# Expert rounds of 32 tokens over four column groups of TensorE, weights in twelve 8 KB ring slots

## The chip, the core and the metric

The kernel runs on one core of one Trainium2 chip. A core has TensorE (PE, with its weight loads listed apart as PEld), VectorE (DVE), ScalarE (ACT), GpSimd (POOL) and SyncE (SP), which here does nothing but issue the transfers of the weights. Everything is float32. The metric is the device time of one execution in microseconds, lower is better.

## What is computed

The reference applies two blocks to 256 tokens of width 1024 (the first block also reads 256 context tokens). Each layer mixes tokens (three kinds of attention-like mixers) and then runs a mixture of experts. There are 32 experts in 4 groups of 8; every token goes to the two best experts of its best group. The first block has one layer, the second has two, so there are three expert phases. Cut to what matters here:

```python
# first block: EXPERT_HIDDEN = 512, two experts of 32 for each of 256 tokens
def expert_block(args):
    xb, e = args
    g, u = jnp.split(xb @ w_up[e], 2, axis=-1)      # 1024 x 1024 weights
    return (jax.nn.silu(g) * u) @ w_down[e]          # 512 x 1024 weights
y = y[dest] * gate ; segment_sum over the tokens
# second block, twice: D_EXPERT = 256, the same choice of two out of 32
hid = jax.nn.silu(t @ w_gate[g, e]) * (t @ w_up[g, e]) * combine   # 1024 x 256 each
y = y + hid @ w_down[g, e]                                         # 256 x 1024
```

All experts' weights are read once in each phase: 32 x 6.29 MB = 201.3 MB in the first block and 32 x 3.15 MB = 100.7 MB in each layer of the second. How many tokens an expert has follows from the inputs and decides how often an expert is run. Worked out from the reference with its own inputs (experts 0 to 31 in order):

| phase | tokens of each expert |
|---|---|
| first block | 2 0 4 1 3 2 7 7 8 6 12 3 0 6 6 7 **37** 20 12 13 7 4 1 0 **129** 14 **40** 2 **108** 29 13 9 |
| second block, layer 1 | 32 14 18 25 20 29 23 1 15 9 12 18 2 6 12 10 28 9 8 7 22 7 17 6 29 19 15 6 5 **36 38** 14 |
| second block, layer 2 | **43** 27 28 **57 54** 25 **33 33** 9 7 14 6 1 8 5 12 6 2 5 5 12 0 6 12 11 22 7 12 5 24 3 18 |

## The kernel before

The program of each engine is written out by hand with semaphores between them. SP streams all weights of the kernel, in the order of their use, through a ring of six slots of 16 KB per partition (2 MB each, 12.6 MB in all). It may refill a slot once PE has counted up `piece_used` for it (`expert_loads`, L452 to L467).

An expert phase (`experts_pe`, `experts_act`, `experts_dve`) is a loop. `batch_of` gives its shape: in the first block a turn takes 2 experts with 64 token places each (16 turns), in the second 4 experts with 32 places each (8 turns a layer). In a turn, DVE makes a 0/1 matrix that picks the tokens (L1090) and its product with the gates (L1096). PE gathers the tokens with four 512-column matmuls (L941), turns the result by eight transposes (L948, L957), and multiplies with up and gate weights (L979). There the tokens are stationary, 64 or 32 columns of the array for each expert, and the weights stream past in 512 columns, so two or four experts share the array side by side. ACT applies silu (L1045), DVE multiplies (L1115), PE transposes the hidden values (L990) and runs the down matmuls (L1006). The results go back to the tokens by four `combine` matmuls (L929), which add into four PSUM banks through the whole phase; they are one round late and sit between the other steps.

An expert with more tokens than places is run again before its main round with the same weights (`each_batch`; the number of extra rounds is loaded from SBUF into a register, L899, and a loop runs over them). In the first block an extra round is for one expert with 128 places; in the second it covers all 4 experts of the turn. By the table there are 2 extra rounds in the first block (experts 24 and 28), 1 in layer 1 and 2 in layer 2 of the second: 37 rounds with the 32 main ones.

A weight piece of a turn is one slot: 4 pieces of up (or gate and up), 2 of down. Each is released by the last matmul that reads it, in the main round.

Of the kernel before, what the change touches and what calls it, by code (L numbers as in the profile page):

```python
# [17 lines left out]
ALU = mybir.AluOpType  # L18
# [3 lines left out]
P = 128  # L22
D = 1024
# [3 lines left out]
SLOT = 4096  # L27
RING = 6
# [3 lines left out]
GRID = 64  # L32
BIG = 1e30
# [119 lines left out]
SEMS = """params loaded_x loaded_ctx loaded_bias bias_out piece0 piece1 piece2 piece3 piece4 piece5 piece_used  # L153
# [6 lines left out]
w_sel w_g0 w_g1 w_ct w_ct_sb w_comb_sb w_up w_silu w_hid w_ht0 w_ht1 w_y w_got_s w_got_v w_gt0 w_gt1 w_xg_v w_xg_s w_ysb_s w_ysb_v w_selg p2_mm p2_s p2_v st_mm pool_w head_s head_v final_gain moe_mm  # L160
fin_x
cq_sq cq_mean cq_sqrt cq_n cq_T cq_Ts q_mm q_sb kv_mm kv_sb head_T 
st_zb st_ln st_x st_a st_T st_Ts st_pv st_o pool_d pool_ds pool_y pool_o
w_hsb0 w_hsb1 const2 params2 written scale lam lam_sums lam_exp router_w zero_tile ranked w_cur c_used """.split()
# [33 lines left out]
class Ring:  # L198
# [5 lines left out]
    def place(self, dmas):  # L204

        slot = self.n % RING
        self.n += 1
        self.loads[slot] += 16 * dmas
        return slot, self.sems[f"piece{slot}"], self.loads[slot]

    def loop(self, turns, per_turn, dmas, dmas_down):

        assert per_turn == RING
        out = []
        for j in range(per_turn):
            slot, step = (self.n + j) % RING, 16 * (dmas if j < 4 else dmas_down)
            out.append((slot, self.sems[f"piece{slot}"], self.loads[slot], step))
            self.loads[slot] += step * turns
        self.n += turns * per_turn
        return out  # L220
# [20 lines left out]
def hybrid_kernel(nc, ins, out):  # L241
# [6 lines left out]
    with ExitStack() as ctx:  # L248
# [5 lines left out]

        ring = sb("ring", RING * SLOT).rearrange("p (r n) -> p r n", r=RING)
        X = sb("X", NT * D).rearrange("p (t d) -> p t d", t=NT)
# [79 lines left out]
        comb_next = arena[:, 13056:13312]  # L336
        cur = work[:, 768:784]
        silu_sb, hid = work[:, 784:1296], work[:, 1296:1808]
        hidT = work[:, 1808:2320].rearrange("p (c n) -> p c n", c=4)
        gotT = work[:, 2320:3344].rearrange("p (k n) -> p k n", k=KD)  # L340
        got = arena[:, 11008:12032]
        y_sb = arena[:, 12032:13056]
# [3 lines left out]
        ranks = rt[:, 0:128].rearrange("p (r e) -> p r e", e=NE)  # L346
# [70 lines left out]
        def w_cols(slot, width):  # L417

            return ring[:, slot, 0:KD * width].rearrange("p (k n) -> p k n", k=KD)

        def start_piece(sp, slot, sem, piece, layer):
# [13 lines left out]
            elif kind in ("wout", "wout2"):  # L435
                w = ins["w_out"][0] if kind == "wout" else ins["w_out_2"][layer]
                sp.dma_start(ring[:, slot, 0:4 * D].rearrange("p (k n) -> p k n", k=4),
                             w[512 * j:512 * j + 512, :].rearrange("(k p) n -> p k n", p=P)).then_inc(sem, 16)
            elif kind == "mla":
                sp.dma_start(ring[:, slot, 0:1536].rearrange("p (k n) -> p k n", k=2),  # L440
                             ins["w_uq_2"][layer].rearrange("(k p) n -> p k n", p=P)).then_inc(sem, 16)
                sp.dma_start(ring[:, slot, 1536:2560], ins["w_ukv_2"][layer]).then_inc(sem, 16)

        up1 = ins["w_expert_up"][0].rearrange("(b e) (k p) n -> b p e k n", e=2, p=P)
        down1 = ins["w_expert_down"][0].rearrange("(b e) (k p) n -> b p e k n", e=2, p=P)

        def expert_loads(sp, plan, which, ups, down):

            nb, _, hidden = batch_of(which)
            base, turns = plan.n, NE // nb  # L450
            slots = plan.loop(turns, RING, 2, hidden // P // 2)
            with sp.Fori(0, turns) as turn:  # L452
                for j, (slot, sem, _, _) in enumerate(slots):

                    sp.wait_ge(sems["piece_used"], turn * RING + (base + j - RING + 1))
                    if j < 4:
                        v = piece_view(slot, which, False)
                        for u, src in enumerate(ups):
                            if which == 2:
# [1675 lines left out]
```

## Time and profile before

| | |
|---|---|
| median of 3 runs | 1836.61 us (1832.91 to 1839.12) |
| profiled execution, its own time | 1836.74 us |
| span of its trace | 1835.0 us |
| PE busy | 1550.9 us (85%) |
| DVE, ACT busy | 453.4 us, 400.8 us |
| weights moved by SP's queue | 468.61 MB |
| first block's experts | from 391.96 us, last combine from 943.73 us |
| second block's experts, layer 1 | from 1118.05 us, last combine from 1377.61 us |
| second block's experts, layer 2 | from 1541.91 us, last combine from 1814.98 us |

The span runs from the first to the last instruction. A fp32 matmul shows as two records for PE (and two for PEld), a transpose as one. "x64" behind a row is the number of such records merged in it; a row's duration covers them all. The ends of matmuls are modelled, so distances between starts are the surer measure.

### The profile page before, as it was taken

How to read it: one execution, taken by the hardware profiler on the slowest of the kernel's cores; microseconds unless marked ns; L12 is line 12 of the kernel's file. 1: busy time of each engine (PE TensorE's matmuls, PEld its weight loads, DVE VectorE, ACT ScalarE, POOL GpSimd, SP SyncE). 2: the span in 40 equal slices, each digit the busy share in tenths (PEclk: the TensorE clock that was granted, in tenths of full speed). 3: DMA queues.
4: the chain of work that ended last, by engine and by line, in shares of the span. 5: the costliest groups of instructions: out<-in, count | busy, mean ns of one | idle time of the engine just before them, and what ended most of it. 6: DMA issues, size and time to landing. Idle time of an engine off the chain costs nothing.

```text
span 1835.0 us, 20256 instructions
## 1 busy us (share of the span) xinstructions
PE 1550.9 (85%) x7433; PEld 705.2 (38%) x7434; DVE 453.4 (25%) x1278; ACT 400.8 (22%) x778; POOL 41.7 (2%) x80
## 2 busy tenths in 40 slices
PE   3999987889999999999979788777788887888674
PEld 2555444343333333333327444222226544332221
DVE  0103356432121212121222513111112523121111
ACT  1101224122222222222222412121212412222111
POOL 2000201000000000000000000000000000000000
PEclk9899969979999999999989888897999997998888
DMA  9857300229999999858582224999975321779995
GB/s 319 308 200 276 114 2 1 105 87 405 410 410 410 410 410 410 344 220 329 220 331 92 92 97 163 397 392 396 393 263 212 138 63 45 275 283 392 395 393 205
DMA packets 174249, 477.30 MB, mean 260 GB/s; under 512 B 8465, under 2 KB 18958, under 8 KB 174014
## 3 DMA queue, kind: packets, MB, share of 16 engines
q1 hardware_dynamic: 171136, 468.61, 66.9%
q0 software_dynamic: 2160, 6.51, 1.3%
q10 hardware_dynamic: 910, 1.59, 0.3%
q8 instruction: 29, 0.48, 0.1%
q14 instruction: 14, 0.11, 0.0%
HBM read 474.71 MB, written 1.97 MB: 260 GB/s over the span
## 4 chain that ended last, share of the span: by engine, by line
PE 66%; DMA 14%; DVE 8%; SPq 7%; issue 2%; ACT 2%; ACTq 0%; DVEq 0%; POOL 0%
PE psum L979 16%; DMA ring<-in_w_down 10%; PE psum L1006 9%; PE psum L929 6%; PE psum L941 6%; SPq L460 6%; PE psum L1638 5%; PE psum L662 5%; PE psum L1634 3%; DMA ring<-in_w_up 2%; PE psum L1208 2%; PE psum L1196 2%; SPq L467 1%; PE psum L542 1%; PE psum L1242 1%
## 5 line engine op out<-in xcount | busy, mean ns | idle before, releaser
L979 PE MATMUL psum<-ring,arena 128*32 128x512 f32 (+2 forms) x2304 | 413.0, 635 | 64.0 <-DMA ring<-in_w_up 62.0
L979 PEld LDWEIGHTS psum<-ring,arena 128*32 128x32 f32 (+2 forms) x2304 | 124.4, 128 | 343.5 <-issue 290.6
L1006 PE MATMUL psum<-ring,arena 128*32 128x512 f32 (+2 forms) x1152 | 211.4, 640 | 52.0 <-DMA ring<-in_w_down 43.3
L929 PE MATMUL psum<-arena 128*128 128x512 f32 x320 | 169.4, 635 | 3.2 <-DVE arena L1069 3.2
L1115 DVE TENSOR_TENSOR arena<-arena,psum 128x256 f32<-128x256 f32 (+1 forms) x37 | 20.4, 551 | 502.5 <-ACT arena L1045 502.5
L941 PE MATMUL psum<-xn,arena 128*128 128x512 f32 x296 | 133.3, 593 | 1.5 <-DVE arena L1090 1.5
L1006 PEld LDWEIGHTS psum<-ring,arena 128*32 128x32 f32 (+2 forms) x1152 | 59.1, 127 | 173.3 <-issue 106.8
L1045 ACT ACTIVATE arena<-psum 128x256 f32<-128x256 f32 (+1 forms) x37 | 18.0, 487 | 411.3 <-PE psum L979 411.3
L1638 PE MATMUL psum<-ring,hT 128*128 128x512 f32 x224 | 97.7, 593 | 0.0
L929 PEld LDWEIGHTS psum<-arena 128*128 128x128 f32 x320 | 54.2, 197 | 100.8 <-issue 95.2
L1067 DVE COPY arena<-psum 128x512 f32<-128x512 f32 x40 | 27.6, 691 | 252.2 <-PE psum L929 252.2
L662 PE MATMUL psum<-ring,arena 128*128 128x512 f32 x192 | 86.0, 607 | 2.4 <-DVE arena L638 1.5
L941 PEld LDWEIGHTS psum<-xn,arena 128*128 128x128 f32 x296 | 56.7, 192 | 74.2 <-issue 71.1
L1031 ACT ACTIVATE arena<-psum 128x512 f32<-128x512 f32 x40 | 23.9, 597 | 214.7 <-PE psum L929 214.7
L1041 ACT ACTIVATE arena<-psum,small 128x128 f32<-128x128 f32 x148 | 48.7, 411 | 97.1 <-PE psum L957 97.1
L1638 PEld LDWEIGHTS psum<-ring,hT 128*128 128x128 f32 x224 | 41.9, 190 | 50.5 <-issue 50.5
L1031 ACT ACT_TABLE_LOAD x37 | 47.5, 1283 | 51.2 <-issue 45.4
L662 PEld LDWEIGHTS psum<-ring,arena 128*128 128x128 f32 x192 | 37.0, 195 | 50.3 <-issue 50.3
L1100 DVE COPY arena<-psum 128x512 f32<-128x512 f32 x37 | 25.6, 692 | 95.0 <-PE psum L941 95.0
L1634 PE MATMUL psum<-hT,ring 128*128 128x256 f32 (+2 forms) x144 | 47.4, 491 | 1.6 <-DVE hT L1913 1.3
L1045 ACT ACT_TABLE_LOAD x37 | 47.5, 1283 | 0.7
L753 PE MATMUL psum<-const_sb,xn 128*128 128x128 f32 x80 | 17.7, 413 | 34.3 <-DVE xn L724 34.3
(329 smaller groups left out, 1441.6 us busy)
## 6 DMA issues: line engine op xcount, KB each, us to landing
ring<-in_w_expert_up SPq DMA_DIRECT2D x128, 1024.0 KB, 9.8
ring<-in_w_expert_down SPq DMA_DIRECT2D x64, 1024.0 KB, 12.2
ring<-in_w_gate SPq DMA_DIRECT2D x64, 1024.0 KB, 14.2
ring<-in_w_up SPq DMA_DIRECT2D x64, 1024.0 KB, 14.3
ring<-in_w_down SPq DMA_DIRECT2D x32, 2048.0 KB, 16.8
ring<-in_w_mod SPq DMA_DIRECT2D x12, 2048.0 KB, 14.6
ring<-in_w_in SPq DMA_DIRECT2D x6, 2048.0 KB, 9.1
ring<-in_w_out SPq DMA_DIRECT2D x6, 2048.0 KB, 13.4
```

What stands on the lines that cost most here:

```text
L460: sp.dma_start(v[:, u], src[bass.ds(turn, 1)][0][:, :, 2 * j:2 * j + 2, :]).then_inc(sem, 16)
L662: mm = pe.matmul(ps[2 * t + n], mix[:, 4 * j + k, P * t:P * t + P], w[:, k, 512 * n:512 * n + 512], start=(j == 1 and k == 0), stop=(j == ...
L929: return pe.matmul(ps[4 + 2 * t + n], comb[:, P * t:P * t + P], y_sb[:, 512 * n:512 * n + 512], start=False, stop=True, skip_group_check=True)
L941: mm = pe.matmul(ps[2 + n], sel[:, t, :], xn[:, t, 512 * n:512 * n + 512], start=(t == 0), stop=(t == NT - 1))
L979: mm = pe.matmul(out_, gotT[:, k, its], rhs, start=(k == 0), stop=(k == KD - 1))
L1006: mm = pe.matmul(ps[n][its, :], hidT[:, k, its], view[:, e, kk, 512 * n:512 * n + 512], start=(k == 0), stop=(k == chunks - 1))
L1031: act.activation(y_sb[:, 0:512], ps[0], ACT.Copy).then_inc(sems["w_ysb_s"], 1)
L1041: ins_ = act.activation(gotT[:, k, :], ps[1][:, P * (k - 4):P * (k - 4) + P], ACT.Identity, scale=scale[:, k:k + 1], bias=0.0 if shift is ...
L1045: act.activation(silu_sb[:, 0:hidden], ps[2][:, 0:hidden], ACT.Silu).then_inc(sems["w_silu"], 1)
L1196: mm = pe.matmul(ps[4 + part][:, S * c:S * c + S], w[:, k, col:col + P], h2T[:, k, :], start=(k == 0), stop=(k == KD - 1))
L1634: mm = pe.matmul(bank[0:m, 0:tokens], w[:, k, col + P * i:col + P * i + m], hT[:, k, 0:tokens], start=(k == 0), stop=(k == KD - 1))
L1638: mm = pe.matmul(bank, hT[:, k, P * i:P * i + P], w[:, k, :], start=(k == 0), stop=(k == KD - 1))
```

## The change

The three expert phases get a new shape. A group is now 4 experts in every phase: one gather of 4 x 32 places for the group, whose 16 matmuls give the tokens' columns at once (no transposes). Within a group the first block runs 4 rounds of one expert, the second block 2 rounds of two. In a round the four 32-column groups of the array hold the same tokens (or two experts' tokens twice) and stream different quarters (halves) of the weights' columns: 32 up matmuls of 256 columns. The down matmuls are 16 of 256 columns, or 8 of 512. The four combine matmuls over all 128 rows become 8 over 32 rows each (first block) or 4 over 64 rows (second). A round has 32 places for each expert in all phases, and an extra round gathers anew for its own expert or pair.

The ring becomes twelve slots of 1 MB. A piece is one transfer: two weight rows of 4 KB per partition, or for gate and up of the second block 8 KB in one run per partition, where the old kernel's runs are 2 KB. In the first block a piece is released as before, by its last matmul; in the second, four at once after the up matmuls and combine, and two after the down matmuls.

```diff
-SLOT = 4096
-RING = 6
+SLOT = 2048
+RING = 12
+ROUND = 6
...
+        def each_round(eng, at, which, extra_round, main_round):
...
+            rounds = GROUP // experts_of(which)
             eng.wait_ge(*at("ranked"))
...
+            with eng.Fori(0, NE // GROUP) as turn:
+                for i in range(rounds):
+                    n = eng.value_load(extra[0:1, bass.ds(turn * rounds + i, 1)], min_val=0, max_val=7)
+                    begin = extra_round(turn, i, None)
                     with eng.If(n > 0):
...
                         with eng.Fori(0, n):
...
+                            extra_round(turn, i, True)
+                    main_round(turn, i)
...
+            def gather(select, width, out):
+
+                for k in range(KD):
+                    for t in range(NT):
+                        mm = pe.matmul(out(k)[:, 0:width], xn[:, t, P * k:P * k + P], select[:, t, 0:width],
+                                       start=(t == 0), stop=(t == NT - 1))
...
+            def combine():
+
+                w, wide = W * at_once, S * at_once
+                for t in range(NT):
+                    for n in range(P // w):
+                        r = slice(w * n, w * n + w)
+                        out_ = ps[4 + n][:, S * t:S * t + S] if which == 1 else ps[4 + 2 * t + n]
+                        mm = pe.matmul(out_, comb[r, P * t:P * t + P], y_sb[r, 0:wide], start=False, stop=True,
+                                       skip_group_check=True)
+                return mm
+
+            def up(turn, i, got, col, main):
...
+                            for j in range(4):
+                                mm = pe.matmul(out_(j), got[:, k, col:col + W], w[:, kk, :, j, :],
+                                               start=(k == 0), stop=(k == KD - 1))
+                        if main and piece < 3:
+                            mm.then_inc(sems["piece_used"], 1)
+                else:
+                    for piece in range(4):
+                        slot_ready(turn, ROUND * i + piece)
...
             def round_(turn, i, got, gates, col, main, ready):
...
                 pe.wait_ge(sems["w_comb_sb"], v + part)
...
+                combine_turn(gates, col)
+                if ready:
+                    pe.wait_ge(sems[ready[0]], ready[1])
+                up(turn, i, got, col, main)
+                pe.wait_ge(sems["w_ysb"], v + part)
+                combine()
+                if main and i == rounds - 1:
+                    gather_group()
                 pe.wait_ge(sems["w_hid"], v)
...
+                pe.transpose(U[:, 0:P], hid, ident).then_inc(sems["w_ht"], 1)
+                if main:
+
+                    pe.sem_inc(sems["piece_used"], 1 if which == 1 else 4)
+                pe.wait_ge(sems["w_hsb"], v)
+                down(turn, i, main)
+                if main:
+
+                    pe.wait_ge(sems["w_y"], v)
+                    pe.sem_inc(sems["piece_used"], which)
```

PE's program in the first block's loop, main round of two experts, before. 64x512 means 64 stationary columns and 512 streamed ones, L941 is the gather, L979 up, L1006 down, L929 combine:

```order
L941 MATMUL psum<-xn,arena 128x512 x4
L948 MATMUL psum<-const_sb,arena 128x128 x4
L952 MATMUL psum<-const_sb,arena 128x128 x2
L957 MATMUL psum<-const_sb,arena 128x128 x4
L929 MATMUL psum<-arena 128x512
...
L979 MATMUL psum<-ring,arena 64x512 x24
L929 MATMUL psum<-arena 128x512 x2
L990 MATMUL psum<-const_sb,arena 128x128 x4
```

The same place now, a main round of one expert (L1026 turns the gates, L984 is up, L971 combine, L1045 the hidden values' transpose, L1015 down):

```order
L1026 MATMUL psum<-const_sb,arena 32x128 [waits w_comb_sb]
L1026 MATMUL psum<-const_sb,arena 32x128 x7
L984 MATMUL psum<-ring,arena 32x256 [waits piece0]
L984 MATMUL psum<-ring,arena 32x256 x7
...
L971 MATMUL psum<-arena 128x256 [waits w_ysb]
L971 MATMUL psum<-arena 128x256 x7
L1045 MATMUL psum<-const_sb,arena 128x128 [waits w_hid]
...
L1015 MATMUL psum<-ring,arena 32x256 x7
L915 ISA [waits w_y]
L915 TENSOR_LOAD extra
```

The gather and its transposes have left the main round (the gather stands in every fourth one), every matmul is narrower, and the round ends in a wait for its own down matmuls (`w_y`) ahead of the load of the next number of extra rounds. An extra round on PE, which stands ahead of it in a loop of its own:

```order
L949 MATMUL psum<-arena,xn 128x32 x16
L1032 ISA
L1026 MATMUL psum<-const_sb,arena 32x128 x8
...
L971 MATMUL psum<-arena 128x256 x8
L1045 MATMUL psum<-const_sb,arena 128x128
L1015 MATMUL psum<-ring,arena 32x256 x16
L920 REGISTER_ALU
```

It holds a gather of its own (L949) and all steps of a main round. The loop's body is four such pairs, 600 matmul calls in a turn of 4 experts; before it was 162 in a turn of 2.

## Rows read from the trace of the kernel before

**Rows 1.** Page, 40 equal slices of the span: GB/s moved

```profile
GB/s 319 308 200 276 114 2 1 105 87 405 410 410 410 410 410 410 344 220 329 220 331 92 92 97 163 397 392 396 393 263 212 138 63 45 275 283 392 395 393 205
```

**Rows 2.** Windows: stretch, length, busy us (records) per engine, PEclk, DMA share, GB/s

```profile
392.00:765.00 373.00, 365.69 (x1532) 138.08 (x1532) 68.18 (x222) 79.24 (x135) 0.00 (x0) 1.00 0.99 397
765.00:796.00 31.00, 30.30 (x81) 13.71 (x82) 5.56 (x18) 7.21 (x15) 0.00 (x0) 1.00 0.25 100
1118.00:1383.00 265.00, 205.55 (x1125) 67.07 (x1123) 43.79 (x132) 51.77 (x101) 0.00 (x0) 0.90 0.95 357
1744.00:1776.00 32.00, 23.41 (x132) 7.50 (x124) 4.70 (x15) 6.00 (x12) 0.00 (x0) 0.89 1.04 395
```

**Rows 3.** Chain of waits, first block's experts: start us, us, what

```profile
459.37 13.95 PE psum L979 x64
...
475.93 7.09 PE psum L1006 x32
...
489.98 2.35 PE psum L979 x9
...
765.51 13.99 PE psum L979 x32
...
795.82 4.50 PE psum L979 x19
```

**Rows 4.** Waits of SP's queue, 459 to 643 us: total us, times, longest

```profile
SPq L463 <- PE psum L979: 82.4, 18, 9.2
```

**Rows 5.** DMA issues, 400 to 460 and 700 to 760 us: KB each, us to landing

```profile
ring<-in_w_expert_up SPq DMA_DIRECT2D x16, 1024.0 KB, 9.0
...
ring<-in_w_expert_up SPq DMA_DIRECT2D x16, 1024.0 KB, 10.7
```

**Rows 6.** DMA view, 1585 to 1807 us in 40 slices: GB/s

```profile
GB/s 387 400 410 135 0 7 366 388 386 391 410 403 386 388 386 397 407 399 387 386 387 400 410 392 388 386 388 406 410 386 387 387 390 407 405 387 386 387 393 412
```

**Rows 7.** Timeline of PE, second block, layer 2, first extra round: start, us

```profile
1541.91 3.60 PE L941 MATMUL psum<-xn,arena 128*128 128x512 f32 x8
...
1547.81 7.07 PE L979 MATMUL psum<-ring,arena 128*32 128x512 f32 x64
...
1556.64 0.38 PE L990 MATMUL psum<-const_sb,arena 128*128 128x128 f32 x2
1557.36 3.64 PE L1006 MATMUL psum<-ring,arena 128*32 128x512 f32 x32 [0.34 <-ACT arena L1049]
```

**Rows 8.** Timeline of PE, modulation matmuls over four column groups

```profile
81.21 3.70 PE L1570 MATMUL psum<-ring,arena 128*32 128x128 f32 x128
```

**Rows 9.** Timeline of PE, matmuls on 64 rows, in two row groups

```profile
985.57 1.68 PE L1221 MATMUL psum<-arena 64*128 64x128 f32 x16
987.18 7.17 PE L1208 MATMUL psum<-ring,hT 128*128 128x256 f32 x32
```

**Rows 10.** Timeline of DVE, experts of the second block

```profile
1596.60 0.42 DVE L1115 TENSOR_TENSOR arena<-arena,psum 128x256 f32<-128x256 f32 x1 [9.04 <-ACT arena L1045]
...
1774.34 0.17 DVE L1084 COPY arena<-arena 128x16 f32 x1 [1.08 <-issue]
```

**Rows 11.** Timeline of SP, layer 2: last transfer ahead of the experts, first in them

```profile
1498.05 14.79 SPq L467 DMA_DIRECT2D ring<-in_w_down  x2
1569.92 0.37 SPq L460 DMA_DIRECT2D ring<-in_w_gate  x1
```

**Rows 12.** Page, DMA queues: packets, MB, share of 16 engines

```profile
q8 instruction: 29, 0.48, 0.1%
q14 instruction: 14, 0.11, 0.0%
```

**Rows 13.** Timeline of PE, the last combine of each expert phase

```profile
943.73 3.67 PE L929 MATMUL psum<-arena 128*128 128x512 f32 x8 [1.08 <-DVE arena L1069]
...
1377.61 3.67 PE L929 MATMUL psum<-arena 128*128 128x512 f32 x8 [1.08 <-DVE arena L1069]
...
1814.98 3.67 PE L929 MATMUL psum<-arena 128*128 128x512 f32 x8 [1.08 <-DVE arena L1069]
```

More of the change, by code:

```diff
@@ L32 @@
 GRID = 64
+GROUP = 4
+W = 32
 BIG = 1e30
@@ L919, in experts_pe, with quadrant @@
+                    main_round(turn, i)
+        def quadrant(j):
+            return slice(W * j, W * j + W)
+        U, Y, G = ps[0], ps[1], (ps[2], ps[3])
         def experts_pe(pe, at, plan, which, part):
             route_pe(pe, at, which)
[L921 to L930 removed]
@@ L932, in round_, with slot_ready @@
-            def round_(turn, last, alone):
-                who = [(e, slice(w * e, w * e + w)) for e in range(nb)] if alone is None else [(alone, slice(0, P))]
+            win, extras, groups = windows["pe"], windows["pe_extras"], windows["pe_groups"]
+            at_once = experts_of(which)
+            rounds = GROUP // at_once
+            slots, step = plan.loop(NE // GROUP, ROUND * rounds)
+            def slot_ready(turn, j):
+                slot, sem, value = slots[j]
+                pe.wait_ge(sem, turn * step + value)
+                return ring[:, slot, :]
@@ L935, in round_, with combine_turn @@
+            def combine_turn(gates, col):
+                for t in range(NT):
+                    w = W * at_once
+                    for o in range(0, P, w):
+                        mm = pe.matmul(U[o:o + w, S + P * t:S + P * t + P], gates[:, t, col:col + w], ident,
+                                       start=True, stop=True)
+                mm.then_inc(sems["w_ct"], 1)
+            def round_(turn, i, got, gates, col, main, ready):
                 pe.reg_add(win, win, 1)
                 v = pe.snap(win)
-                pe.wait_ge(sems["w_sel"], v)
@@ L1026, in experts_act, with gathered @@
-            hidden = batch_of(which)[2]
-            def outputs(value):
-                act.wait_ge(sems["w_y"], value)
-                act.activation(y_sb[:, 0:512], ps[0], ACT.Copy).then_inc(sems["w_ysb_s"], 1)
-            def round_(turn, last, alone):
+            win, groups = windows["act"], windows["act_groups"]
+            rounds = GROUP // experts_of(which)
+            wide = S if which == 1 else 512
+            def gathered():
+                act.reg_add(groups, groups, 1)
+                act.wait_ge(sems["w_g1"], act.snap(groups))
+                for k in range(4, KD):
+                    ins_ = act.activation(gotT[:, k, :], G[1][:, P * (k - 4):P * (k - 4) + P], ACT.Identity,
+                                          scale=scale[:, k:k + 1], bias=0.0 if shift is None else shift[:, k, 0:1])
+                ins_.then_inc(sems["w_xg_s"], 1)
@@ L1731, in _ @@
             at = Tally(sems)
-            windows["act"] = counter(act, "window_act")
+            for name in ("act", "act_groups"):
+                windows[name] = counter(act, f"window_{name}")
             def link(ins):
```

496 lines of the change are left out of this document (247 added, 249 removed).

## The prediction

> **What bounds the kernel now.** I read the slices first: the expert phases show as three plateaus near 410, 395 and 395 GB/s, with holes in them [rows 1]. The windows then say that both PE and the DMA engines are full in the first block's phase (PE busy 365.7 of 373 us, DMA share 0.99), and that in an extra round the DMA falls to 100 GB/s [rows 2]. The chain of waits names only PE there: a turn takes 489.98 - 459.37 = 30.61 us, an extra round 795.82 - 765.51 = 30.31 us [rows 3], and SP waits for PE's up matmuls, not PE for data [rows 4]. But the time from issue to landing of the same 1 MB creeps from 9.0 to 10.7 us in 300 us [rows 5]. So the transfers fall behind by up to 0.17 us in a turn of 30.61 us while the slices stand at 410 GB/s [rows 1]: 12.58 MB in 30.6 to 30.8 us is all that they can do, and I use 409.8 GB/s. The first block's experts are PE's by name and the DMA's within 0.3%: halving PE's work cannot make a turn shorter. What can go are the holes, where PE works on extra rounds and SP may not refill.
>
> In the second block the DMA leads: 395 GB/s at PE busy 23.4 of 32 us [rows 2]. The slices inside swing between 386 and 410 GB/s [rows 6]: gate and up come in 2 KB runs, down in 4 KB runs. Two holes remain: at 1605 us behind an extra round [rows 6], and in layer 2 from before the experts' start until 1569.92 us, when the first slot comes free [rows 11].
>
> **Prices of the new steps.** The up stage of four column groups: 7.07 us for 64 records of 512 columns [rows 7], so 3.5 us at 256. Down in the same way 3.64 / 2 = 1.8 us. Turning the gates is 16 records of 128 columns in four column groups; 128 such took 3.70 us [rows 8], so 0.46 us. The hidden values' transpose, copy and start of down: 1557.36 - 1556.64 = 0.72 us [rows 7]. The gather: like L941 8192 streamed column passes, 3.45 us by the distance of its neighbours, and as much when only 32 columns stream, since its 32 weight loads of 128 columns remain; without them it would be under 2 us, a gain that I keep as the lower end.
>
> The combine has no twin: 16 records on 32 rows in four row groups, or 8 on 64 rows in two. The nearest row is L1221, where two row groups alternate in pairs: 16 records start-to-start 987.18 - 985.57 = 1.61 us [rows 9], although their columns one after another would be 4 x (0.22 + 0.44) = 2.6 us at the rate of L979. So row groups overlap. Fully side by side the new combine is 0.9 us, one after another 3.4 us; I take 1.7 us, the measured 0.1 us per record. The Trainium skill's page TensorE: Matmul & The Clock Gate ("Packing small matmuls") says that weight loads overlap running matmuls only where the row groups differ, and gives 3.07 times for four row groups; the trace's pairs agree that they overlap. By that factor the combine would be 3.4 / 3.07 = 1.1 us, an estimate from that page.
>
> Then the round's end. PE now waits for its own down matmuls and loads the number of extra rounds with an empty queue. The trace shows that price on DVE alone: 1.08 us with nothing waited for between two register-loaded parts [rows 10]; with the wait, 1.4 us. Bounds: 0.3 and 3 us.
>
> - Main round M: 0.46 + 3.5 + 1.7 + 0.72 + 1.8 = 8.2 us, with the end 9.6 us; plus 3.45 us in the last round of a group.
> - Extra round X: gather 3.45, DVE's scaling of it 0.42 and its semaphores (with the shift of the first block) 1.2, up 3.5, combine 1.7, 0.72, down 1.8: 12.4 us. Between two extra rounds about 1.0 us more, since DVE makes the next selection only after its copy of the turned gates.
>
> The DMA's price of an expert of the first block is 6 x 1.0486 MB / 409.8 GB/s = 15.35 us. For a round of the second, gate and up in 8 KB runs: not in the trace; 2 KB runs give 386 and 4 KB runs 410, a fixed part per run carried on gives at most 423; I take 415, so 15.2 us (bounds 14.9 and 15.35). Against 15.35 us, M with its share of the gather is 10.4 us: between extra rounds the DMA sets the pace everywhere, and PE's savings are hidden.
>
> **What the extra rounds become.** With 32 places the first block needs 1 for expert 16 (37 tokens), 4 for expert 24 (129), 1 for expert 26 and 3 for expert 28 (108): 9 instead of 2, each 12.4 instead of 30.3 us. Layer 1 needs 2 (rounds 14 and 15) instead of 1, layer 2 needs 4 (rounds 0 to 3) instead of 2, against about 20 us each before (from L941 to the end of L1006 it is 19.1 us [rows 7]). Six of twelve slots hold the weights in use, so an extra round of 12.4 us alone fits under the 15.35 us in which the other six fill. A chain of them does not.
>
> *First block.* PE starts up at about 395 us (3 us earlier, no transposes), gives back the first slot at 396, and with 2.3 us from release to data the pieces of expert 24 are all there at 396 + 2.3 + 23 x 15.35 = 751.4. From there PE sets the time: 0.9 (half a down), 3 x (1.0 + 12.4), main 8.2 = 800.7; expert 25 9.6; expert 26 1.4 + 12.4 + 8.2; expert 27 9.6 + 3.45; expert 28 1.4 + 3 x 12.4 + 2 x 1.0 + 8.2; experts 29 and 30 19.2; expert 31 13.1: 926.4 us. Before, this point was 942.7 (1.08 us ahead of the last combine) [rows 13]: -16 us.
>
> *Layer 1.* The first four slots come back only after up and combine, at 1130 instead of 1126. From 1132 the DMA brings 14 rounds x 15.2 = 213, until 1345. Rounds 14 and 15 each with an extra one: round 14's pieces are there at 1330, its extra round ends at 1332.5, main at 1340.7, then 1.4 + 12.4 + 8.2 + 3.45 = 1366.2; 2 us for the waits of both on the pieces: 1368. Before 1376.5: -8 us. *Layer 2.* First extra gather at 1548.4 (group gather from 1541.9, 3.45, then DVE's scaling, register load and selection, about 3); rounds 0 to 3 are PE's: 20.6, 1.4 + 24.1, 22.0, 25.5 = 1642. Round 3's slots come back at about 1639.8, so rounds 5 to 15 arrive by 1642 + 11 x 15.2 = 1809.6, and the last round ends 6 us later, 1815.7. Before 1813.9: +2 us. The last combine is 2 us shorter each time but DVE's residual no longer overlaps it: -1 us in all.
>
> I add 4 us for code loading (below): 1836.7 - 16 - 8 + 2 - 1 + 4 = 1817.7, so **1818 us**. The profiled execution's 1836.74 us is the median of the runs, 1836.61.
>
> **The rivals.**
> *A. The combine is quicker.* At 0.9 us the 28 rounds that PE sets (16 in the first block, 4 in layer 1, 8 in layer 2) save 0.8 us each: about 1797 us. The overlap in [rows 9] speaks for it, the loads of 128 columns against it.
> *B. The rounds are dearer than their sum (slower side).* PE's sequencer meets 28 rounds with waits that no row shows: PE's empty queue after `w_y`, and DVE's chain ahead of each extra gather. With 2.4 instead of 1.4 us at the end, 1.5 between extra rounds and 1 us more in X, the three phases become +4, -4 and +9: 1846 us. It decides from 0.7 us per round on. If row groups did not overlap for 32 rows, combine 3.4 us, the same rounds cost 1.7 us each: 1875 us.
> *C. The code of the loop.* PE's loop in the first block grows from 162 to 600 matmul calls, at four instructions a call (load and matmul, twice) from about 560 to 2,380. Before, the instruction queue carried 29 and 14 packets in the whole run although the loops turned 32 times [rows 12], so loops were not fetched again. If the jump over each unused extra round (324 instructions) now waits 2.5 us for code, the DMA-paced part hides it (10.4 + 2.5 < 15.35), and experts 25 to 31 pay about 15: 1830 us. If it waits 8 us behind the weights' queue, as 1 MB waits 9 [rows 5], every expert takes 18.4 us: about 1930 us. The Trainium skill, Runtime: NRT & Kernel Launch ("Instruction fetch mechanics"), gives PE 2048 instructions of memory in blocks of 256 and says that a taken branch outside what is loaded stalls. The body is above that figure; no row shows such a stall.
> *D. The DMA-paced rounds leave PE half idle and its clock at 1.2 GHz.* It was 0.89 to 0.90 in the second block's phases [rows 2]. At half clock M is 17 us and above the DMA's 15.35, but then PE is busy throughout, and busy stretches have shown 1.00 [rows 2]. 1850 us at most.
>
> **Chances.** Main sum 43%, A 13%, B 20% (7% of it the full 3.4 us combine), C 19% (5% the dear form), D 5%. What this kernel's measurement can tell from no change is 0.3%, or 5.5 us. Faster by more: 0.40 of the main sum, A, 0.05 of the rest: 58%. Within it: 11%. Slower: 31%. The range leaves out A's far end, the 3.4 us combine's and the dear code's: 1788 to 1862 us; the main sum alone has 1806 to 1831.
>
> **What will show it.** In the first block until expert 24 the DMA at 410 GB/s and 15.35 us between gathers of one expert each (61.4 us between the group gathers); PE idle behind DMA waits there. The chain should name the DMA up to about 751 us and PE after it. The combine's 16 records tell A and B apart, the gap from the last down matmul to the next gate turning tells the 1.4 us, and the instruction queue's packets tell C (29 before). In the second block the GB/s must rise above 400 in the steady part. I am wrong if the DMA's pace in the first block changes, if an extra round is not 12 to 14 us, or if rounds 0 to 3 of layer 2 do not end near 1642.

## The result

| | before | after |
|---|---|---|
| median of the runs, us | 1837.2 (4 runs, 1832.9 to 1839.1) | 1984.4 (4 runs, 1977.7 to 1992.8) |
| span of the profiled execution, us | 1835.0 | 1986.5 |
| experts, block 1, us | 554.8 | 696.1 |
| experts, layer 1 / layer 2 of block 2, us | 262.6 / 276.2 | 264.4 / 283.2 |

The change makes the kernel slower: the ratio is 1.0807, 95% interval 1.0757 to 1.0857. I had forecast 1818 us, in the range 1788 to 1862. The time of an expert phase is counted here, and in all that follows, from the first gather's start to the last combine matmul's start. Block 1 gives 141 of the 147 us of the difference; layer 1 stands near before, and layer 2 is 7 us longer.

### The profile after

On the page of the changed kernel, the granted clock and the GB/s in 40 slices, the instruction queue and the chain's shares (answers to [rows 1, 12]):

```profile
PEclk9999789787877787789797888898988987989988
...
GB/s 324 313 219 202 68 0 46 70 397 345 317 363 339 263 337 319 365 0 270 240 182 303 112 85 89 197 418 418 418 366 188 128 57 85 141 241 389 418 418 189
...
q8 instruction: 118, 1.93, 0.4%
...
PE 61%; issue 15%; DMA 10%; DVE 6%; ACT 2%; PEld 2%; SPq 1%; ACTq 0%; DVEq 0%; PEldq 0%; POOL 0%
```

The plateau at 410 GB/s in block 1 is gone (263 to 365 now), while block 2's rose from 395 to 418. The instruction queue carried 118 packets in place of 29. "Issue", time in which PE waits for nothing that the profile shows, is 15% of the chain.

Windows of the changed kernel: block 1's experts, a steady part of layer 1, all of layer 2 (columns as in [rows 2]):

```profile
390.00:1080.00 690.00, 451.10 (x5841) 277.58 (x5845) 63.30 (x205) 69.67 (x171) 0.00 (x0) 0.81 0.75 288
...
1685.00:1967.00 282.00, 233.98 (x2358) 132.29 (x2356) 35.33 (x117) 44.98 (x106) 0.00 (x0) 0.93 0.77 313
1300.00:1450.00 150.00, 111.61 (x1126) 59.07 (x1126) 15.47 (x50) 23.08 (x55) 0.00 (x0) 0.90 1.02 418
```

In block 1 PE is busy 65% of the time and the DMA engines 75%: neither is full any more, where both were [rows 2]. So each waits for something else. PE's waits there, 380 to 1082 us (what waited, for what: us in total, times, longest):

```profile
PE psum L1026 <- issue: 160.4, 27, 10.8
PE psum L984 <- issue: 32.6, 8, 4.2
PE psum L949 <- issue: 26.1, 4, 9.6
```

They sum to 219 us. No wait for a transfer of weights stands beside them (the next in size is 16.3 us, 41 short waits for ACT). L1026 turns the gates, the first matmul behind a round's end. PE's timeline shows three main rounds:

```profile
523.10 1.93 PE L1015 MATMUL psum<-ring,arena 128*32 128x256 f32 x32 [0.45 <-ACT arena L1106]
534.82 1.08 PE L1026 MATMUL psum<-const_sb,arena 128*32 128x128 f32 x16 [9.78 <-issue]
535.67 5.95 PE L984 MATMUL psum<-ring,arena 128*32 128x256 f32 x64
541.55 1.15 PE L971 MATMUL psum<-arena 32*128 32x256 f32 x16
542.63 0.33 PE L1045 MATMUL psum<-const_sb,arena 128*128 128x128 f32 x1
543.32 1.93 PE L1015 MATMUL psum<-ring,arena 128*32 128x256 f32 x32 [0.36 <-ACT arena L1106]
546.88 0.64 PE L1026 MATMUL psum<-const_sb,arena 128*32 128x128 f32 x16 [1.62 <-issue]
547.33 1.04 PE L984 MATMUL psum<-ring,arena 128*32 128x256 f32 x15
552.50 5.38 PE L984 MATMUL psum<-ring,arena 128*32 128x256 f32 x49 [4.12 <-issue]
...
559.66 1.93 PE L1015 MATMUL psum<-ring,arena 128*32 128x256 f32 x32 [0.45 <-ACT arena L1106]
568.90 1.08 PE L1026 MATMUL psum<-const_sb,arena 128*32 128x128 f32 x16 [7.30 <-issue]
```

Between the last down matmul and the next gate turning, where the untaken extra body lies, stand 9.8, 1.6 and 7.3 us; where it is 1.6, a gap of 4.1 us follows inside the up stage, behind 15 of its 64 matmuls, at a place where nothing is waited for. After the gap of 9.8 us the up stage takes 5.95 us for what takes 3.64 us in e1 below; after the one of 4.1 us its last 49 matmul records alone take 5.38 us. The granted clock is 0.50 there (the lower level, 1.2 GHz) from 534.8 to 539 us and from 552.5 to 555 us, both times behind the gap, and 1.00 from 541.5 to 546 us. The combine (L971) is 1.15 us.

The DMA view says what goes on in these gaps. First its line for the gap of 9.8 us (window 525.04:534.82), then for the turn of four experts from one group gather to the next (518.7:594.0):

```profile
q8 instruction: 2, 0.03, 1.3%
...
q8 instruction: 11, 0.18, 1.0%
```

The gaps of 4.1 and 7.3 us have one packet of this queue each. In block 1 PE has 30 "issue" waits of over 2.5 us, and in each one or two packets of the queue start; a turn without extra rounds has eleven. In the kernel before, the queue carries nothing at all from 430 to 940 us.

In block 2's layer 2, an extra round of the changed kernel and what follows:

```profile
1690.89 3.78 PE L949 MATMUL psum<-arena,xn 128*128 128x64 f32 x32 [1.71 <-ACT arena L1096]
1694.60 0.66 PE L1026 MATMUL psum<-const_sb,arena 128*64 128x128 f32 x8
1695.84 3.66 PE L996 MATMUL psum<-ring,arena 128*32 128x256 f32 x64 [0.58 <-DVE arena L1156]
1699.43 1.99 PE L971 MATMUL psum<-arena 64*128 64x512 f32 x8
1701.35 0.33 PE L1045 MATMUL psum<-const_sb,arena 128*128 128x128 f32 x1
1702.04 1.92 PE L1008 MATMUL psum<-ring,arena 128*32 128x512 f32 x16 [0.37 <-ACT arena L1106]
1703.90 0.66 PE L1026 MATMUL psum<-const_sb,arena 128*64 128x128 f32 x8
...
1714.00 2.22 PE L949 MATMUL psum<-arena,xn 128*128 128x64 f32 x18 [1.39 <-issue]
```

The extra round is 13.0 us from gather to gate turning (forecast 12.4), the main round 10.1 us with its end (forecast 9.6).

### The profile page after: what moved, and what is told of

The parts are those of the page before. It is cut to its first block, busy times and chain, and to the rows that moved or that the text cites. A ratio compares the mean times of both kernels' runs of the same rounds, so it can differ in the third digit from the quotient of the medians.

```text
span 1986.5 us, 32398 instructions
## 1 busy us (share of the span) xinstructions
PE 1487.3 (75%) x13232; PEld 888.7 (45%) x13233; DVE 400.3 (20%) x1118; ACT 331.4 (17%) x748; POOL 41.6 (2%) x80
## 3 DMA queue, kind: packets, MB, share of 16 engines
q8 instruction: 118, 1.93, 0.4%
## 4 chain that ended last, share of the span: by engine, by line
PE 61%; issue 15%; DMA 10%; DVE 6%; ACT 2%; PEld 2%; SPq 1%; ACTq 0%; DVEq 0%; PEldq 0%; POOL 0%
PE psum L984 11%; DMA ring<-in_w_up 8%; PE psum L949 7%; PE psum L1729 5%; PE psum L676 4%; PE psum L971 4%; PE psum L996 4%; PE psum L1015 4%; PE psum L1725 2%; PE psum L1026 2%; PE psum L1008 2%; PE psum L1286 2%; PE psum L1298 1%; PEld psum L996 1%; PE psum L556 1%
## 5 line engine op out<-in xcount | busy, mean ns | idle before, releaser
L984 PE MATMUL psum<-ring,arena 128*32 128x256 f32 x2624 | 216.2, 494 | 35.2 <-issue 32.6
L1026 PE MATMUL psum<-const_sb,arena 128*32 128x128 f32 (+1 forms) x960 | 63.3, 340 | 207.6 <-issue 203.5
L949 PE MATMUL psum<-arena,xn 128*128 128x128 f32 (+2 forms) x1344 | 177.0, 294 | 35.8 <-issue 34.1
L949 PEld LDWEIGHTS psum<-arena,xn 128*128 128x128 f32 x1344 | 170.4, 209 | 60.7 <-issue 60.7
L996 PE MATMUL psum<-ring,arena 128*32 128x256 f32 x2432 | 168.4, 439 | 29.0 <-DMA ring<-in_w_up 27.4
L984 PEld LDWEIGHTS psum<-ring,arena 128*32 128x32 f32 x2624 | 110.8, 143 | 129.1 <-issue 103.8
L1026 PEld LDWEIGHTS psum<-const_sb,arena 128*32 128x32 f32 (+1 forms) x960 | 38.3, 139 | 250.7 <-issue 248.4
L1104 ACT ACTIVATE arena<-psum 128x128 f32<-128x128 f32 x79 | 21.9, 277 | 717.7 <-PE psum L984 468.9
L996 PEld LDWEIGHTS psum<-ring,arena 128*32 128x32 f32 x2432 | 90.0, 126 | 97.2 <-issue 64.8
L971 PE MATMUL psum<-arena 32*128 32x256 f32 (+1 forms) x992 | 127.7, 470 | 2.1 <-ACT arena L1110 2.1
L1015 PE MATMUL psum<-ring,arena 128*32 128x256 f32 x1312 | 79.3, 382 | 16.3 <-ACT arena L1106 16.3
L1008 PE MATMUL psum<-ring,arena 128*32 128x512 f32 x608 | 73.1, 598 | 15.8 <-ACT arena L1106 15.8
L971 PEld LDWEIGHTS psum<-arena 32*128 32x128 f32 (+1 forms) x992 | 58.1, 185 | 57.1 <-issue 51.9
L1015 PEld LDWEIGHTS psum<-ring,arena 128*32 128x32 f32 x1312 | 39.0, 110 | 45.0 <-ACT arena L1106 13.9
L1106 ACT ACTIVATE arena<-psum 128x128 f32<-128x128 f32 x79 | 21.9, 277 | 200.3 <-PE psum L1045 200.3
```

Of the source, the lines that this page charges most:

```text
L949: mm = pe.matmul(out(k)[:, 0:width], xn[:, t, P * k:P * k + P], select[:, t, 0:width], start=(t == 0), stop=(t == NT - 1))
L971: mm = pe.matmul(out_, comb[r, P * t:P * t + P], y_sb[r, 0:wide], start=False, stop=True, skip_group_check=True)
L984: mm = pe.matmul(out_(j), got[:, k, col:col + W], w[:, kk, :, j, :], start=(k == 0), stop=(k == KD - 1))
L996: mm = pe.matmul(out_(j), got[:, k, col + W * e:col + W * e + W], w, start=(k == 0), stop=(k == KD - 1))
L1008: mm = pe.matmul(Y[quadrant(j), :], hidT[:, W * src:W * src + W], pair[e][:, half, 512 * n:512 * n + 512], start=(half == 0), stop=(half = ...
L1015: mm = pe.matmul(Y[quadrant(j), 0:S], hidT[:, W * k:W * k + W], w[:, kk, S * j:S * j + S], start=(k == 0), stop=(k == 3))
```

## The experiments

Theory C: PE's program for a turn of block 1 (some 2,380 instructions, 560 before) doesn't stay at hand, and jumps in it wait for code. Its rivals were W, the round's end (own wait and register load), and D, the clock as a cause of its own. Engines' lines in a variant are its own: L1027 of e1 is L1026 of the changed kernel, and so on.

**e1, two experts a turn.** The same bodies, waits and transfers, 16 turns in place of 8:

```diff
+GROUP_OF = {1: 2, 2: 4}
...
-            rounds = GROUP // experts_of(which)
+            rounds = GROUP_OF[which] // experts_of(which)
...
-            with eng.Fori(0, NE // GROUP) as turn:
+            with eng.Fori(0, NE // GROUP_OF[which]) as turn:
```

> The changed kernel, its first block in 16 turns of two experts in place of 8 of four (each group gather for 64 places); TensorE's program for a turn is then some 1,165 instructions in place of 2,380. All bodies for tokens over 32, all waits and all transfers stay. Theory C (the program of a turn is too long to stay at hand, and each skip over an unused body is fetched anew): the 7 to 11 us of 'issue' ahead of the gate turns of block 1 fall to 2 us or less, packets of the instruction queue in block 1 from 86 to under 20, the experts of block 1 from 689 us to 530-560, the whole from 1984 to 1820-1860. Theory W (what costs is the end of a round: the wait for the own down matmuls and the register load): the gaps stay, 1980 or more, since 8 more group gathers are added. Theory D (the clock at 1.2 GHz is the cause, not the result): likewise no less than 1970.

Measured: 1849.9 us, ratio to before 1.0077 (1.0047 to 1.0107); 37 packets of the instruction queue in the run, block 1's experts 558.1 us. PE's waits in block 1, the page's GB/s, and a window of its middle:

```profile
PE psum L1027 <- issue: 45.1, 27, 2.2
PE psum L985 <- DMA ring<-in_w_expert_up: 26.0, 23, 1.5
```

```profile
GB/s 323 325 177 271 114 1 1 106 147 410 410 409 409 410 409 410 259 231 315 167 381 137 50 93 178 419 418 418 417 273 124 91 106 1 274 233 417 418 418 173
```

```profile
450.00:740.00 290.00, 215.31 (x2965) 128.85 (x2958) 31.18 (x117) 42.48 (x107) 0.00 (x0) 0.91 1.03 410
```

The longest gap ahead of a gate turn falls from 10.8 to 2.2 us, the DMA is back at 410 GB/s, and 138 us of block 1 are gone, although eight group gathers were added. C holds; W and D, with all their waits and the same matmuls still there, don't explain it.

**e2, the same code with few bytes.**

```diff
+                    if light:
+                        dst, src = dst[:, 0:1, 0:S], src[:, 0:1, 0:S]
                     sp.dma_start(dst, src).then_inc(sem, 16)
```

> The changed kernel with the transfers of block 1's expert weights cut to 1 KB of the 8 KB in each partition (the rest of a slot keeps old data, so block 1's numbers mean nothing); the count of transfers, all instructions and all waits stay. Theory C with a dear queue (a fetch waits behind the weights in the 16 engines): the gaps ahead of the gate turns fall from 7-11 us to 2-4, block 1's experts take 450-520 us, the whole 1750-1820. Theory C with a price of its own (a fetch takes so long whatever else moves): the gaps stay at 7-10 us, block 1's experts 640-690 us. Theory W or D: gaps stay too, with no more packets of the instruction queue than in the kernel before.

Measured: 1915.5 us (one run), block 1's experts 600.5 us, with 57 GB/s in place of 288, and again 118 packets, eleven in a turn. PE's waits in block 1:

```profile
PE psum L1028 <- issue: 110.7, 27, 7.7
PE psum L951 <- issue: 17.5, 4, 5.4
...
PE psum L986 <- issue: 13.7, 8, 2.1
```

The three "issue" sums are 142 us in place of 219; e1 has 57, nearly all at the rounds' ends. So about 85 us are the fetches' own, and about 77 more come with the weights' traffic on the same DMA engines. Both forms of C were half right, and block 1's 600.5 us lie between the two forecasts.

**e3 to e6, e9, e10, e13, e14: dead code in the kernel before.** Ahead of the extra bodies of block 1 an untaken one is put, with N matmuls of four instructions each:

```diff
                     n = eng.value_load(extra[0:1, bass.ds(at_, 1)], min_val=0, max_val=7)
+                    if dead and which == 1:
+                        with eng.If(n > 6):
+                            for _ in range(dead):
+                                eng.matmul(ps[0][:, 0:P], ident, ident, start=True, stop=True)
                     with eng.If(n > 0):
```

In e9 and e13 it stands ahead of the first extra body alone (`and alone == 0`), in e14 there, five times over.

> The kernel before, with an untaken body of 112 matmuls (some 450 instructions) ahead of each of the two extra bodies of a turn of block 1; a turn is then 1,460 instructions in place of 560, with two more skips. Theory C with a bound on the turn's length near 2,000: nothing is fetched, 1837 within 0.5%. If every skip costs, whatever the turn's length: 2 x 16 more gaps of 7 us, of which what the wait for weights does not cover shows, 1860-2050.

> The same with 225 matmuls in each untaken body (some 900 instructions); a turn is 2,366 instructions, near the changed kernel's 2,380. Theory C: 3 to 4 gaps of 7-10 us in each of 16 turns, partly under the wait for weights; packets of the instruction queue over 60 in block 1; 1900-2100. Theories W and D: 1837 within 1%, since no round end and no matmul of the executed path is changed.

> The kernel before, with 160 untaken matmuls (640 instructions) ahead of each of the two extra bodies of a turn of block 1: the turn is some 1,840 instructions. If what counts is that the turn stays at hand as a whole, and the bound lies near 2,000: 1833 to 1853, as with 1,460 instructions, block 1's experts 555-560 us, some 30 packets of the instruction queue in the whole run. If the price rises with the length skipped: between the 1,460 and the 2,366 run, 1950-2050.

> The same with 190 matmuls each: a turn of some 2,080 instructions. With a bound just under it: 18-23 us of issue ahead of a batch and about 168 packets, 2150-2200, nearly as with 2,366; with a price by length: 2000-2100; with a bound between 2,080 and 2,366: 1833-1853.

> The kernel before with all 320 untaken matmuls in one body, ahead of the first extra body of a turn; the turn has the same 1,840 instructions as e5, but one long skip less. If each transfer of control to instructions that are not at hand has one price: the gap ahead of a batch falls from 22 us to about 15 (two such places, the skip and the jump back, in place of three), the whole from 2197 to about 2080. If the price goes by the instructions of the turn, which are all fetched anew: 22 us and 2190-2200 again.

> The kernel before with 136 untaken matmuls (544 instructions) in each of the two bodies: a turn of some 1,650 instructions, between 1,460 (1853, nothing fetched) and 1,840 (2197, 22 us a batch). It only places the bound: 1833-1853 if it lies above, 2150-2200 if below; nothing between is expected.

> The kernel before with one untaken body of 1,000 matmuls (4,000 instructions) ahead of the first extra body: a turn of some 4,560 instructions, twice the changed kernel's, with one long skip, of which no turn touches more than the 560 instructions it runs and what is fetched ahead. If blocks touched decide: as e9, 1835-1850, under 40 packets of the instruction queue. If the length of the turn decides (over 2,048 instructions): 15 us or more ahead of each batch, 2080 or more, over 100 packets.

> The turn of 1,840 instructions of e9 with its 1,280 untaken ones cut into five bodies of 256, one behind the other: each skip lands in the next block of 256 instructions, so every block of the turn is touched, and with those fetched ahead of each they are more than eight. If blocks touched decide: dear, as e5 and e10, over 100 packets, 2050-2250. If only the length of the turn or a few long skips decide: as e9, 1835-1855.

Measured, one run each (the kernel before beside them 1832 to 1836; packets are the page's instruction queue, the gap is the longest "issue" wait ahead of a batch in block 1):

| | untaken instructions | turn, instructions | packets | gap, us | block 1, us | time, us |
|---|---|---|---|---|---|---|
| before | none | 560 | 29 | none | 554.8 | 1837.2 |
| e3 | 2 x 450 | 1,460 | 33 | once 10.6 | 557.5 | 1852.6 |
| e10 | 2 x 544 | 1,650 | 169 | 22.7 | 912.9 | 2208.9 |
| e5 | 2 x 640 | 1,840 | 169 | 23.1 | 906.7 | 2197.2 |
| e6 | 2 x 760 | 2,080 | 168 | 23.0 | 901.9 | 2192.1 |
| e4 | 2 x 900 | 2,366 | 168 | 22.9 | 903.3 | 2194.8 |
| e9 | 1 x 1,280 | 1,840 | 32 | once 8.5 | 556.9 | 1842.2 |
| e13 | 1 x 4,000 | 4,560 | 31 | once 6.2 | 557.4 | 1837.2 |
| e14 | 5 x 256 | 1,840 | 184 | 29.3 | 1010.5 | 2311.1 |

The timeline of PE at the end of a batch in e5, in e14 and in e9 (last combine of the batch, next gather):

```profile
651.83 1.13 PE L933 MATMUL psum<-arena 128*128 128x512 f32 x2
675.79 6.65 PE L945 MATMUL psum<-xn,arena 128*128 128x512 f32 x8 [22.83 <-issue]
```

```profile
623.01 1.13 PE L933 MATMUL psum<-arena 128*128 128x512 f32 x2
653.32 1.22 PE L945 MATMUL psum<-xn,arena 128*128 128x512 f32 x1 [29.18 <-issue]
```

```profile
640.31 1.12 PE L933 MATMUL psum<-arena 128*128 128x512 f32 x2
641.27 3.60 PE L945 MATMUL psum<-xn,arena 128*128 128x512 f32 x8
```

Not one of these instructions is ever executed, and they cost up to 475 us. C stands by itself, without the changed kernel. Several of my expectations fell here: e3 lies just above its 0.5%, e5 outside both of its ranges, e4 and e14 are dearer than their ranges (1900 to 2100, 2050 to 2250), e10 9 us above its dear one. The price doesn't rise with the length (e10, e5, e6 and e4 agree within 17 us), and the length of the turn is not the bound: 1,650 instructions are dear and 4,560 are free. e9 fell outside both of its expectations, and led to the rule that e13 and e14 tested: what counts is how many blocks of code a turn touches. A packet of the queue is 1.93 MB / 118 = 16.4 KB. e13 fetched 2 packets more than the kernel before in spite of 4,000 more instructions: what is skipped in one leap isn't fetched. In a turn of e5 (window 620.5:675.8), then in one of e14 (653.3:714.4), the DMA view counts:

```profile
q8 instruction: 9, 0.15, 1.3%
...
q8 instruction: 10, 0.16, 1.1%
```

A turn of e4, e6 and e10 has 9 as well, one of the changed kernel 11; from 430 to 940 us e3, e9, e13 and the kernel before have none, e1 has one. What a turn touches is either kept whole or fetched anew whole: nothing lies between 33 and 168 packets. The Trainium skill, Runtime: NRT & Kernel Launch ("Instruction fetch mechanics"), gives PE room for 2048 instructions in a FIFO of blocks of 256, so eight blocks; 9, 10 and 11 fetched in the dear turns agree with that, and e9 and e13 show that it is blocks touched, not the body's length, that has to stay within it. The runs alone place the bound below nine blocks fetched in a turn; that it is eight and not seven is the Trainium skill's. An estimate by the Trainium skill's blocks agrees: lay out a turn by the lengths above, with 156 instructions for each unused extra body, and count for each landing its own block and the next. Then e9 and e13 touch 6 or 7 blocks, e3 7 or 8, e4, e5, e6 and e10 7 to 9 (by where the turn begins in a block), e14 9 or 10. The same section speaks of "only 2 cache lines"; the run of 560 instructions over 16 turns with 29 packets in all speaks against it.

The price goes by the fetches. In e5's gap (652.96 to 675.79 us) six packets of the instruction queue start, in e14's (624.14 to 653.32) seven: 3.8 and 4.2 us of waiting for each. In the last 9 us of e14's gap the core moves 5 GB/s, the fetches alone, and they start 3.1 to 3.5 us apart: they come one by one even with the DMA engines free. What a block costs that is fetched ahead only, and isn't waited for, stays open.

e3 and e9 are single runs, 19 and 8 us above before, while their phases of block 1 stand at +3 and +2; the rest lies outside of them and I leave it open.

**e7, no wait for the own down matmuls.** e1, and:

```diff
+                if main:
+                    mm.then_inc(sems["piece_used"], which)
+                    mm = (pe.matmul(Y[0:W, S:S + 4], ident[:, 0:W], ident[:, 0:4], start=True, stop=True) if which == 1 else
+                          pe.matmul(Y[0:W, 0:4], zeros[:, 0:W], ident[:, 0:4], start=False, stop=True,
+                                    skip_group_check=True))
                 mm.then_inc(sems["w_y"], 1)
...
-                if main:
-
-                    pe.wait_ge(sems["w_y"], v)
-                    pe.sem_inc(sems["piece_used"], which)
```

The small matmul has 4 columns and writes a free part of the bank, or adds zeros to it.

> Two experts a turn (as e1), and TensorE no longer waits for its own down matmuls at a main round's end: the last of them hands the pieces back itself and a small matmul behind it tells ScalarE. If the 1.4-2.0 us ahead of each gate turn are that wait: they fall to 0.5 or less, which shows where TensorE sets the pace (some 8 main rounds at the end of block 1, 8 to 12 in layer 2, few in layer 1), 15 to 30 us in all, 1820-1835. If they are the register load and the branch alone: 1.4 us stay, 1845-1850, no change from e1.

Measured: 1827.4 us, ratio to before 0.9953 (0.9936 to 0.997), 22 us under e1 and the fastest of all kernels here that compute everything. The experts take 546.3, 255.0 and 280.2 us. PE's timeline at a round's end:

```profile
650.07 1.93 PE L1016 MATMUL psum<-ring,arena 128*32 128x256 f32 x32 [0.45 <-ACT arena L1109]
651.81 0.20 PE L1022 MATMUL psum<-const_sb 128*32 128x4 f32 x2
652.32 0.64 PE L1032 MATMUL psum<-const_sb,arena 128*32 128x128 f32 x16 [0.31 <-issue]
```

0.31 us are left of 1.3 to 2.2: the cost was the wait. Register loads and branches are all still there, and show no more than that behind it.

**e8, the extra counts read early.** e7, and:

```diff
+                ns = [eng.value_load(extra[0:1, bass.ds(turn * rounds + i, 1)], min_val=0, max_val=7)
+                      for i in range(rounds)]
                 for i in range(rounds):
-                    n = eng.value_load(extra[0:1, bass.ds(turn * rounds + i, 1)], min_val=0, max_val=7)
+                    n = ns[i]
```

> As e7, and every engine reads the extra counts of all rounds of a turn at the turn's start. If the register load is the rest of the gap ahead of a gate turn: all but the first gap of a turn fall to 0.2-0.6 us, 5 to 15 us less than e7 (1810-1830). If the branches are it: as e7 within 0.3%.

Measured: 1835.5 us, ratio 0.9999 (0.9982 to 1.0015), so 8 us more than e7 and against both expectations. In block 1 12 of the gate turns wait for "issue", 11 of them 1.0 to 1.1 us (12.3 us in all; 5.3 in e7), and the phase is 7 us longer. These gaps come once in a turn: two loads in a row at its start are no longer covered, one ahead of each round is.

**e11 and e12, block 2 without extra rounds**, in the kernel before and in e7:

```diff
-                    with eng.If(n > 0):
+                    with eng.If(n > (0 if which == 1 else 6)):
```

> The kernel before, with block 2's extra rounds never taken (tokens beyond 32 places are left out there, so block 2's output is not the reference's; the code stays). Layer 1 has one extra round, layer 2 two: 20 us each where TensorE sets the pace. If the transfers set block 2's pace: layer 1 unchanged (263 us), layer 2 276 -> 255-262.

> e7 (two experts a turn, no wait at the end) with block 2's extra rounds never taken in the same way; these are two in layer 1 and four in layer 2. If the new block 2 is held at 418 GB/s (in place of 395) and its extras alone ate the gain: both layers 245-252 us, against 255 and 280 with them, and 10 to 15 us below e11's. If the rounds themselves are slower than the transfers: no less than e11's layers.

Measured (one run each): before 242.0 and 242.9 us, 1780.5 in all; e7's rounds 238.4 and 239.2 us, 1774.8 in all. Both expectations were missed: layer 1 of the kernel before was not to change and lost 21 us, since its one extra round stands in the last turn, where no transfer covers it; and 418 in place of 395 GB/s gave 4 us a layer and not 10. The end shows where it went. PE in e11, then in e12, end of layer 1:

```profile
1345.75 1.92 PE L1006 MATMUL psum<-ring,arena 128*32 128x512 f32 x16 [3.22 <-DMA ring<-in_w_down]
...
1349.81 3.67 PE L929 MATMUL psum<-arena 128*128 128x512 f32 x8 [1.08 <-DVE arena L1069]
```

```profile
1331.28 6.13 PE L997 MATMUL psum<-ring,arena 128*32 128x256 f32 x64 [6.33 <-DMA ring<-in_w_up]
1337.35 1.99 PE L972 MATMUL psum<-arena 64*128 64x512 f32 x8
...
1346.26 1.99 PE L972 MATMUL psum<-arena 64*128 64x512 f32 x8 [0.74 <-ACT arena L1113]
```

Counted from the phase's start, e12's last wait for weights ends at 222 us and e11's at 235; behind it e11 has 7 us to its last combine matmul (the eighth of the row, at 1352.9), e12 has 16 (at 1347.7): the new up stage needs all four gate and up pieces before its first matmul, and then takes 6.13 us, with the granted clock at 0.50 until 1335 us, behind 6.3 us of idle time. So 13 us are won by the transfers, and 9 given back behind the last of them. The extra rounds then cost e7 16.6 and 41.1 us (two and four of them), before 20.6 and 33.3 (one and two).

## Why the prediction was wrong

**The step that failed** is the claim that between extra rounds the DMA sets the pace everywhere in block 1, through the term "+4 us for code loading". The claim rested on a wait of 2.5 us at each unused extra round, hidden under the DMA's 15.35 us; the waits were 7.5 us, and with them an expert takes 18.5 us. The term measured about 135 us (134.5 us between the medians of e1 and after, 138 us in block 1). I had the right mechanism as rival C, with the packets of the instruction queue as its sign, and priced its dear form at 8 us a jump, "every expert takes 18.4 us: about 1930 us". From 444.64 to 666.43 us, three turns without extra rounds, an expert takes 221.8 / 12 = 18.5 us. So that price was right, in part by luck: the "issue" waits are 7.5 us of it, with the round's end in them, where I had 8 + 1.4; and PE's own work is 10.6 us where I had 9.0, since the granted clock is 0.79 there. What was wrong was the addition: 32 x 18.4 + 9 x 12.4 = 700 us for block 1 (696.1 measured) is 146 us above before and makes about 1975 us of the whole. I gave the dear form 5%, since the loops before had been fetched once [rows 12]. But 29 packets for a turn of 560 instructions say nothing on a turn of 2,380: the row lay on the other side of a bound, and the price between its sides is a step, not a slope. One more sum was off: with the 3.4 us combine the same 28 rounds give 1818 + 28 x 1.7 = 1866, not 1875.

**What held once the code stayed (e1, e7).** The pace of 409.8 GB/s: the slices stand at 409 and 410 until the heavy experts. The round's end: 1.4 us forecast, 1.3 to 2.2 measured in block 1 of e1, 45.1 / 27 = 1.7 in the mean. The extra round with its distance to the next: 13.4 us forecast; in e1, block 1:

```profile
761.46 3.76 PE L950 MATMUL psum<-arena,xn 128*128 128x32 f32 x32
765.15 0.75 PE L1027 MATMUL psum<-const_sb,arena 128*32 128x128 f32 x16
766.28 4.96 PE L985 MATMUL psum<-ring,arena 128*32 128x256 f32 x64 [0.38 <-DVE arena L1164]
771.17 1.15 PE L972 MATMUL psum<-arena 32*128 32x256 f32 x16
...
774.81 3.76 PE L950 MATMUL psum<-arena,xn 128*128 128x32 f32 x32
```

That is 13.35 us, but by luck in part: combine 1.15 in place of 1.7 (rival A was nearer; the 1.1 us estimated from the Trainium skill's page TensorE: Matmul & The Clock Gate agrees), and up 5.0 in place of 3.5. The granted clock is 0.50 in the first 1.7 us of this up stage; why it falls here isn't shown, since in layer 2 of e7 an up stage behind the same wait of 0.4 us for DVE takes 3.66 us. The gather with 32 columns is as dear as with 128, as forecast: 3.69 us to its neighbour (3.45 forecast).

**The phases.** Against my -16, -8 and +2 us, after has +141, +2 and +7, e1 +3, 0 and +10, and e7 -8.5, -7.6 and +4. e1 is the changed kernel without the fetches in every turn, and it stands nearer to rival B (+4, -4 and +9, 1846 us in all) than to the main sum: 1850 us, 32 above my 1818. So B, the dearer rounds, was the second thing that I had too small. Part of the 32 us is e1's own: two of its eight further group gathers lie behind expert 24, 2 x 3.79 = 7.6 us. In layer 2, rounds 0 to 3 were to take 100 us; they took 109 in after, 104 in e7. And I had 6 us behind the last weights; e12 has 16 us behind its last gate or up piece, of which some 11 lie behind its last down piece (an estimate: 2 x 1.05 MB at 418 GB/s are 5 us). e7 comes near my sum only by leaving out the wait at the round's end, which I had counted in. Rival D, the clock alone, has nothing for it: e1 has the clock at 0.91 in its DMA-paced part, and the DMA keeps its pace there.

A round of the second block was to take 15.2 us, with 415 GB/s for the 8 KB runs. The mix of them with the down pieces' 4 KB runs measured 418 GB/s, 15.05 us a round.

## What to carry to other kernels

Before unrolling a hardware loop further, count the blocks of code (16 KB each) that one turn of it touches, skipped bodies included where a skip lands in the next block or two. At nine and more, each turn fetched all of them here, at 20 to 30 us a turn. Gather rarely taken code in one place with one long leap over it, or shorten the turn; the page's instruction queue and the chain's share of "issue" tell which side one is on. And a number from a small loop is no evidence on a large one: ask on which side of the bound the row was taken.

## Not expected of the hardware

- Untaken code costs time: eight versions of dead code moved the kernel before between 1837 and 2311 us.
- It is a step: 2 x 450 untaken instructions cost 3 us in block 1, 2 x 544 cost 358.
- The fetches of code come one by one, with 3.8 to 4.2 us of waiting for each 16.4 KB (e5, e14), and 3.1 to 3.5 us from one to the next with nothing else moving. The weights' traffic makes them dearer: the same fetches cost 85 us with 57 GB/s of it and 162 us with 288.
- Transfers with two thirds of their bytes in runs of 8 KB in each partition, the rest in 4 KB, move 418 GB/s; with 2 KB in place of 8 KB 395.
- Four row groups of 32 rows: 16 combine matmuls in 1.15 us; two of 64 rows: 8 of twice the columns in 1.99 us.
